# Opening of an expert stage: router products taken from x, ranks in five products, token lists made by one-hot products

## Reference, cut to what matters

```python
def hierarchical_moe(h, w_rg, b_rg, w_re, b_re, w1, w3, w2):
    b, s, d = h.shape
    t = h.reshape(b * s, d)
    p_group = jax.nn.softmax((t @ w_rg + b_rg).astype(jnp.float32), axis=-1)
    g_val, g_idx = lax.top_k(p_group, 1)
    fine = (t @ w_re + b_re).astype(jnp.float32).reshape(-1, N_EXPERT_GROUPS, EXPERTS_PER_GROUP)
    fine_sel = jnp.take_along_axis(fine, g_idx[:, :, None], axis=1)[:, 0]
    e_val, e_idx = lax.top_k(jax.nn.softmax(fine_sel, axis=-1), TOP_K_IN_GROUP)
    ...
    for e in range(N_EXPERTS):
        y_e = (jax.nn.silu(t @ w1[e]) * (t @ w3[e])) @ w2[e]
        out = out + combine[:, e:e + 1] * y_e
```

## Time and profile before

| | us |
|---|---|
| median of 3 runs | 3279.79 |
| lowest and highest | 3277.72, 3288.72 |
| the profiled execution, device time | 3293.47 |
| its span, first to last instruction | 3291.5 |
| mean clock granted to PE in it, share of full speed | 0.939 |
| PE busy, share of the span | 90% |
| DVE, ACT, POOL | 51%, 37%, 5% |

### The profile page before, as it was taken

How to read it: one execution, slowest core, us unless ns; L and a number is a source line. 1 busy time by engine, 2 the same in 40 slices (tenths; PEclk the granted TensorE clock), 3 DMA queues, 4 the chain that set the end, 5 groups by cost and what they waited for, 6 DMA issues and landing times. The chain is left out here.

```text
span 3291.5 us, 37902 instructions
## 1 busy us (share of the span) xinstructions
PE 2946.6 (90%) x14197; PEld 2339.0 (71%) x14197; DVE 1693.6 (51%) x2383; ACT 1212.7 (37%) x1625; POOL 172.2 (5%) x131
## 2 busy tenths in 40 slices
PE   7899989789999899897999999989877878599996
PEld 3674776678888888675777887867655567477775
DVE  5444423644677343434654343352466453588886
ACT  2320222323322232432334442244324322377774
POOL 0000001100011000000000000000000100222220
PEclk9999998899999999997999999999979788799998
DMA  8300110021345142110012222223100023599996
GB/s 353 126 26 13 52 51 1 30 86 66 123 148 179 59 134 96 39 45 16 1 34 88 96 96 70 89 70 89 52 8 1 0 66 140 206 364 358 357 343 237
DMA packets 76312, 362.81 MB, mean 110 GB/s; under 512 B 13428, under 2 KB 17347, under 8 KB 50596
## 3 DMA queue, kind: packets, MB, share of 16 engines
q1 hardware_dynamic: 62404, 327.69, 28.1%
q0 software_dynamic: 13792, 33.58, 3.0%
HBM read 360.68 MB, written 16.27 MB: 115 GB/s over the span
## 5 line engine op out<-in xcount | busy, mean ns | idle before, releaser
L305 PE MATMUL ps<-rounded,rounded 128*128 128x512 f32 (+3 forms) x3700 | 1381.5, 373 | 140.0 <-DVE rounded L2238 23.9
L306 PE MATMUL ps<-rounded,rounded 128*128 128x512 f32 (+3 forms) x3700 | 1341.2, 362 | 0.0
L307 PE MATMUL ps<-rounded,rounded 128*128 128x512 f32 (+3 forms) x3700 | 1338.9, 362 | 0.0
L305 PEld LDWEIGHTS ps<-rounded,rounded 128*128 128x128 f32 (+1 forms) x3700 | 708.6, 192 | 324.5 <-issue 120.9
L307 PEld LDWEIGHTS ps<-rounded,rounded 128*128 128x128 f32 (+1 forms) x3700 | 709.7, 192 | 107.7
L306 PEld LDWEIGHTS ps<-rounded,rounded 128*128 128x128 f32 (+1 forms) x3700 | 710.9, 192 | 94.9
L284 DVE TENSOR_TENSOR rounded<-work,rounded 128x1024 fp32r<-128x1024 f32 (+3 forms) x224 | 306.6, 1370 | 838.5 <-ACT rounded L280 838.3
L280 ACT CAST rounded<-work 128x1024 fp32r<-128x1024 f32 (+3 forms) x224 | 261.0, 1166 | 740.1 <-PE ps L307 627.2
L3470 DVE TENSOR_TENSOR rounded<-work,rounded 128x2048 fp32r<-128x2048 f32 x138 | 309.7, 2286 | 77.9 <-ACT rounded L3315 77.9
L3315 ACT CAST rounded<-work 128x2048 fp32r<-128x2048 f32 x138 | 259.4, 1915 | 80.0 <-PE ps L307 80.0
L291 PE MATMUL ps<-cst 128*128 128x256 f32 x466 | 127.6, 435 | 64.6 <-PEq L171 64.6
(11 more groups left out here) (481 smaller groups left out, 2509.4 us busy)
## 6 DMA issues: line engine op xcount, KB each, us to landing
work<-in_moe SPq DMA_DIRECT2D x138, 1024.0 KB, 7.4
work<-in_ffn_up SPq DMA_DIRECT2D x44, 1024.0 KB, 4.8
work<-in_ffn_down SPq DMA_DIRECT2D x66, 512.0 KB, 3.4
work<-in_ada_w SPq DMA_DIRECT2D x12, 2048.0 KB, 17.9
work<-in_ada_w POOLq DMA_DIRECT2D x48, 512.0 KB, 4.0
work<-in_w_out SPq DMA_DIRECT2D x16, 512.0 KB, 3.6
work<-in_w_gates SPq DMA_DIRECT2D x16, 512.0 KB, 3.6
work<-in_w_in_hy SPq DMA_DIRECT2D x12, 512.0 KB, 3.5
```

What stands on the lines that cost most here:

```text
L305: k.nc.tensor.matmul(out, sh, mh, start=start, stop=False)
L306: k.nc.tensor.matmul(out, sh, ml, start=False, stop=False)
L307: return k.nc.tensor.matmul(out, sl, mh, start=False, stop=stop)
```

## The change

1. Router. The 32 products read x as it lies in SBUF, with the router's weights multiplied by the norm's gain (one DVE operation, semaphore `weighted`); the scale of each token is applied to the 20 results (four operations). `h_turned`, its 32 transposes and 8 copies go.
2. Ranks. Five products over all blocks at once, one with the triangle and four with ones, in place of 14.
3. Lists. DVE marks for each pick its tile (`at_tile`) and its position (`at_pos`) as one-hot matrices; eight products of these, summed in PSUM, are the turned list. The list in HBM, its fill, the eight indirect stores, the load and a transpose go.
4. Order on DVE. The gain rows and the normed rows of blocks 0 and 1 come after the picks, those of blocks 2 and 3 after the matching. The table of overflow tiles is made in the loop ahead of tile 2, the shares ahead of tile 3.
5. ACT rounds the first four chunks before the exponentials. POOL empties all four `picked` places itself, ahead of the gathers. SP waits for the table (`mapped`) only at the first overflow tile and for `indexed` no more.
6. Fillers: 8 ahead of the rank products, 8 after them, 16 after the list products.

```diff
@@ SP
             sp.dma_start(w, k.dram["w_router"]).then_inc(asked, 16)
-            sp.wait_ge(cleared, 1)
-            sp.dma_start(slot_rows, by_tile).then_inc(filled, 16)
...
                 sp.dma_start(k.h_rows[a * P:(a + 1) * P, :], h_tok[:, a, :]).then_inc(stored, 16)
-            sp.wait_ge(spread_out, 16 * 8)
-            sp.dma_start(by_tile, slot_rows).then_inc(listed, 16)
-            sp.wait_ge(indexed, 1)
...
+                    if part == 0 and t == N_EXPERTS:
+                        sp.wait_ge(mapped, 1)
@@ POOL
-            pool.wait_ge(counted, 4)
-            pool.wait_ge(filled, 16)
-            pool.wait_ge(numbered, 1)
-            for c in range(8):
-                pool.indirect_dma_start(k.slot_list, bass.IndirectOffsetOnAxis(ap=slot_no[:, c:c + 1], axis=0),
-                                        token_no[:, c:c + 1], None).then_inc(spread_out, 16)
+            for b in range(2, PICKED):
+                pool.memset(picked[b], 0.0).then_inc(emptied, 1)
+            pool.wait_ge(logit, 1)
+            for b in range(2):
+                pool.memset(picked[b], 0.0).then_inc(emptied, 1)
+            pool.wait_ge(emptied, PICKED)
             pool.wait_ge(indexed, 1)
             pool.wait_ge(stored, 64)
...
-            for b in range(2):
-                gather(b)
-            for b in range(2, PICKED):
-                pool.memset(picked[b], 0.0).then_inc(emptied, 1)
-            pool.wait_ge(emptied, PICKED - 2)
-            for b in range(2, PICKED):
+            for b in range(PICKED):
                 gather(b)
@@ PE
+            pe.wait_ge(weighted, 1)
             pe.wait_ge(tok_kept[0], 2)
-            pe.wait_ge(tok_kept[1], 2)
+            for a in range(4):
+                for d in range(DT):
+                    last = nc.tensor.matmul(k.bank(2, 20, 20 * a), k.x[:, d, CTX + a * P:CTX + (a + 1) * P],
+                                            w[:, d * 20:(d + 1) * 20], start=d == 0, stop=d == DT - 1)
+            last.then_inc(logit, 1)
...
+            keep_running(k, 8, 4)
             pe.wait_ge(chosen, 1)
-            flat = picks.rearrange("p a g e -> p a (g e)")
-            for a in range(5):
-                for b in range(min(a, 3) + 1):
-                    last = nc.tensor.matmul(k.bank(1, 16, 16 * a), k.const("s_le_t") if b == a else every, flat[:, b, :],
-                                            start=b == 0, stop=b == min(a, 3))
+            flat = picks.rearrange("p a g e -> p (a g e)")
+            nc.tensor.matmul(k.bank(6, 64, 64), every, flat, start=True, stop=True)
+            nc.tensor.matmul(k.bank(6, 64), k.const("s_le_t"), flat, start=True, stop=False, skip_group_check=True)
+            for a in range(1, 4):
+                last = nc.tensor.matmul(k.bank(6, 64 - 16 * a, 16 * a), every, flat[:, 0:64 - 16 * a], start=False, stop=a == 3,
+                                        skip_group_check=True)
             last.then_inc(summed, 1)
-            pe.wait_ge(listed, 16)
-            nc.tensor.transpose(k.bank(2, EXPERT_TILES), by_tile, k.cst[0:EXPERT_TILES, CAT["ident"]:CAT["ident"] + EXPERT_TILES]
-                                ).then_inc(list_turned, 1)
+            keep_running(k, 8, 4)
+            pe.wait_ge(matched, 1)
+            for c in range(8):
+                last = nc.tensor.matmul(k.bank(3, EXPERT_TILES), at_pos[:, c, :], at_tile[1][:, c, :], start=c == 0, stop=c == 7)
+            last.then_inc(listed, 1)
+            keep_running(k, 16, 4)
@@ DVE
+            dve.wait_ge(asked, 16)
...
+            V.tensor_tensor(by_part, by_part, gains, ALU.mult).then_inc(weighted, 1)
...
+            dve.wait_ge(gain_spread, 1)
+            V.tensor_copy(gain_rows, k.ps[:, 0:D]).then_inc(gained, 1)
...
+            normed_rows(0, 2)
...
+            link(V.tensor_tensor(beyond, slots.unsqueeze(2).to_broadcast(shape), borders.unsqueeze(1).to_broadcast(shape), ALU.is_ge))
+            link(V.tensor_reduce(tile_of, beyond, AX.X, ALU.add))
+            link(V.tensor_tensor(at_tile[0], beyond[:, :, 0:EXPERT_TILES], beyond[:, :, 1:EXPERT_TILES + 1], ALU.subtract))
+            link(V.scalar_tensor_tensor(out=pos, in0=tile_of, scalar=-1.0 * SLOTS, in1=slots, op0=ALU.mult, op1=ALU.add))
+            link(V.tensor_tensor(at_tile[1], at_tile[0], token_no.unsqueeze(2).to_broadcast([P, 8, EXPERT_TILES]), ALU.mult))
+            V.tensor_tensor(at_pos, pos.unsqueeze(2).to_broadcast([P, 8, SLOTS]),
+                            pos_no.unsqueeze(1).to_broadcast([P, 8, SLOTS]), ALU.is_equal).then_inc(matched, 1)
+            normed_rows(2, 2)
...
+                if t == 2:
+                    map_tiles()
+                if t == 3:
+                    shares()
```

More of the change, by code:

```diff
@@ L3090, in experts @@
     ids, off = room(EXPERT_TILES), room(EXPERT_TILES)
-    by_tile = k.row[0:EXPERT_TILES, 0:SLOTS]
-    slot_no, to_row, from_row, rows_of = (
-        k.whole[:, 0:8], k.whole[:, 8:8 + EXPERT_TILES], k.whole[:, 32:32 + EXPERT_TILES],
+    at_tile = [k.words(at + a * EXPERT_TILES * 8, at + (a + 1) * EXPERT_TILES * 8).rearrange("p (c i) -> p c i", i=EXPERT_TILES)
+               for a in range(2)]
+    at += 2 * EXPERT_TILES * 8
+    beyond = k.words(at, at + 8 * (EXPERT_TILES + 1)).rearrange("p (c i) -> p c i", i=EXPERT_TILES + 1)
+    at += 8 * (EXPERT_TILES + 1)
+    borders, pos_no = k.words(at, at + EXPERT_TILES + 1), k.words(at + EXPERT_TILES + 1, at + EXPERT_TILES + 1 + SLOTS)
+    at_pos = k.words(ring.end, ring.end + 8 * SLOTS).rearrange("p (c s) -> p c s", s=SLOTS)
+    tile_of, pos = room(8), room(8)
+    to_row, from_row, rows_of = (
+        k.whole[:, 8:8 + EXPERT_TILES], k.whole[:, 32:32 + EXPERT_TILES],
         k.whole[:, 56:56 + 6 * OVER].rearrange("p (o c) -> p o c", c=6))
@@ L3206, in _ @@
             last.then_inc(gain_spread, 1)
-            for a in range(4):
-                pe.wait_ge(normed, a + 1)
-                if a == 0:
-                    for h in range(2):
-                        pe.wait_ge(tok_kept[h], 4)
-                for d in range(DT):
-                    last = nc.tensor.transpose(k.bank(d, P, a * P), h_tok[:, a, d * P:(d + 1) * P], ident)
-            last.then_inc(back_turned, 1)
-            pe.wait_ge(asked, 16)
-            for a in range(4):
-                for d in range(DT):
-                    if a == 0:
-                        pe.wait_ge(back_kept[d % 2], d // 2 + 1)
-                    last = nc.tensor.matmul(k.bank(0, 20, 20 * a), h_turned[:, d, a * P:(a + 1) * P],
-                                            w[:, d * 20:(d + 1) * 20], start=d == 0, stop=d == DT - 1)
@@ L3301, in _ @@
             nc.scalar.activation(root, sum_sq, ACT.Sqrt, bias=k.const("eps"), scale=1.0 / D).then_inc(rooted, 1)
-            act.wait_ge(back_turned, 1)
-            for d in range(0, DT, 2):
-                nc.scalar.copy(h_turned[:, d, :], k.bank(d)).then_inc(back_kept[0], 1)
-            act.wait_ge(spaced, 1)
-            nc.scalar.activation(g_exp, g_exp, ACT.Exp).then_inc(raised, 1)
-            act.wait_ge(spaced, 2)
-            nc.scalar.activation(gap, gap, ACT.Exp).then_inc(raised, 1)
             def high(c, n):
@@ L3326, in _ @@
             high(0, ring.SPLIT)
+            act.wait_ge(spaced, 2)
+            nc.scalar.activation(g_exp, g_exp, ACT.Exp).then_inc(raised, 1)
+            nc.scalar.activation(gap, gap, ACT.Exp).then_inc(raised, 1)
             for half in range(2):
@@ L3371, in _ @@
                 V.tensor_copy(x_tok[:, a, 0:512], k.bank(2 * a)).then_inc(tok_kept[0], 1)
-            for b in range(2):
-                V.memset(picked[b], 0.0).then_inc(returned, 1)
-            dve.wait_ge(gain_spread, 1)
-            V.tensor_copy(gain_rows, k.ps[:, 0:D]).then_inc(gained, 1)
-            dve.wait_ge(gained, 1)
             dve.wait_ge(rooted, 1)
@@ L3379, in _, with normed_rows @@
             dve.wait_ge(inverse, 1)
[L3380 to L3389 removed]
+            def normed_rows(a, n):
+                for a in range(a, a + n):
+                    V.scalar_tensor_tensor(out=h_tok[:, a, :], in0=x_tok[:, a, :], scalar=root[:, a:a + 1], in1=gain_rows,
+                                           op0=ALU.mult, op1=ALU.mult).then_inc(normed, 1)
             first = k.const("first").unsqueeze(1).to_broadcast([P, 4, 4])
@@ L3400, in _ @@
             dve.wait_ge(logit, 1)
-            bias = k.vec[:, COL["b_router"]:COL["b_router"] + 20].unsqueeze(1).to_broadcast([P, 4, 20])
-            link(V.tensor_tensor(logits, k.bank(0, 80).rearrange("p (a n) -> p a n", n=20), bias, ALU.add))
+            bias = k.vec[:, COL["b_router"]:COL["b_router"] + 20]
+            for a in range(4):
+                last = V.scalar_tensor_tensor(out=logits[:, a, :], in0=k.bank(2, 20, 20 * a), scalar=root[:, a:a + 1], in1=bias,
+                                              op0=ALU.mult, op1=ALU.add)
+                link(last)
             groups = logits[:, :, 0:4]
@@ L3450, in _ @@
```

(7 more changed lines are left out.)

92 lines of the change are left out of this document (46 added, 46 removed).

## The result

| | before | with the change |
|---|---|---|
| median of 6 runs each, us | 3282.3 (3277.72 to 3301.5) | 3261.03 (3253.51 to 3269.76) |
| ratio, 95% interval | | 0.9916 (0.9888 to 0.9944) |
| profiled execution / its span, us | 3293.47 / 3291.5 | 3258.2 / 3256.1 |
| mean granted clock of the span | 0.939 | 0.948 |

A forecast was written before the change was run, and what follows sets the result against it. TensorE, busy 90% of the span, was taken as the bound, with 67.03 us before the loop begins. Opening −22.6, fillers −0.7 and table +1.0 gave −22.3 us, from median 3279.79 to 3257.5 us; range 3249 to 3270.

The forecast's parts named there:

- Steps 1 to 7: Opening of the last stage, from the first transposes at 2758.27 to the indices ready at 2792.4.
- step 1: Opening: router products directly behind the 3.70 us of transposes, taking 10.89 us, end 2772.9; 12.9 us gone.
- step 3: Picks to ranks: PE gain product 1.88, eight fillers 5.21, rank products 2.2; DVE copy and normed rows 3.6; both end 2782.2.
- Step 6: PE sums the lists with eight products in 2.7 us, end 2791.3, replacing indirect stores, load and one transpose.
- Step 8: Stores of normed rows before the gathers: last takes 3.5 us, lands 2794.5 and releases the gathers; other bound 10.9 us.
- rival B: Opening: stores or gathers meet the weight chunks, stores 7.4 us later; −15 us, 3265; chance 0.13.
- Step 9: First gather: 0.8 us from release to start, 7.36 to the transposes, at 2802.7 instead of 2825.30: −22.6 us.
- Step 10: Start of the loop: 16 more fillers let first transposes and products find the higher clock; −0.7 us, bounds 0 and −2.
- Step 11: Overflow table, 3.76 us on DVE, moves into the loop before the third tile's subtractions; +1.0 us, bounds 0 and 3.8.
- A: PE stays on the lower clock in the opening, ranks 3.5 us later; −17 us, 3263; chance 0.15.
- C: Slower: the loop holds PE at the lower clock after the new opening; two tiles give +15 us, 3295; chance 0.03.
- D: Nothing moves: the loop is bound by transfers (share 0.98) and the last chunk sets the end; 3280; chance 0.03.

The follow-up runs named there:

- the list part alone: Kernel before with only one-hot matrices and eight products in place of the list in HBM; opening 61.0 us, first two tiles 38.4 us.
- the kernel with the table early: Changed kernel with the overflow table made before the loop, between normed rows and indices, not ahead of the third tile; opening 44.1 us, stage 506.6 us.

## Why the prediction was right, and where not

The sum was −22.3 us for the stage, and the profile shows −28.8; the medians moved by −21.3, between runs of one kernel that scatter by 24 before and 16 with the change. The timetable, in us from the start of the stage:

| step | | forecast | measured |
|---|---|---|---|
| 1 | router products done, logits at VectorE | 14.6 | 14.4 |
| 2 | picks | 20.2 | 20.25 |
| 3 | VectorE free for the ranks | 23.9 | 23.8 |
| 4 | slots | 27.3 | 27.1 |
| 5 | matched | 30.3 | 30.1 |
| 6 | list summed | 33.0 | 33.4 |
| 7 | indices | 34.1 | 34.45 |
| 8 | last store landed | 36.2 | 35.3 |
| 9 | first gather starts | 37.1 | 36.2 |
| 9 | first transposes | 44.4 | 42.5 |

**Steps 1 to 7** were right to 0.4 us over 34, most taken from a row of the same shape. Five one-hot operations of 184 to 192 columns or fewer took 0.17 to 0.36 and the wide one 1.22, the value of a normed row. Part of it is luck. In step 1 the clock: 10.73 us of router products where the same shape took 8.4 to 12.8 elsewhere. In step 3 two sizes were off and cancelled: the gain product took 3.40 us and not 1.88, the fillers 3.62 and not 5.21. Step 6 was 0.4 late in all, because the list products ran at 0.50 from 2784 on:

```profile
2780.00:2782.00 2.00, 0.09 (x1) 0.10 (x1) 1.90 (x5) 0.00 (x0) 0.00 (x0) 1.00 0.00 0
2782.00:2784.00 2.00, 2.00 (x12) 2.00 (x12) 2.00 (x2) 0.00 (x0) 0.00 (x0) 0.60 0.07 27
2784.00:2786.00 2.00, 2.00 (x9) 1.82 (x9) 0.97 (x5) 0.00 (x0) 0.00 (x0) 0.50 1.00 406
```

(columns as in the earlier trace rows: stretch, busy PE, PEld, DVE, ACT, POOL, clock, DMA share, GB/s).

**Step 8** was mis-sized: 2.7 us for a store, not 3.5; rival B's 10 us did not come, since no chunk was in the queue. Its bold sentence, that the stores release the gathers, is true of the start of the first issue and false of its end, which is what counts: where the issue begins inside the first subtraction, as here, it ends 0.9 to 1.0 behind it.

**Step 9** kept the 7.36 of before. The span from gather start to transposes is no constant: it holds the wait for the subtraction and the traffic of the chunk that SP asks for behind it. In the kernel before the gather started 0.9 after the subtraction did, the issue took 2.30 and the transfer 5.06; with the change it started 1.8 after it, and the two took 1.45 and 4.80, thus 6.25. The earlier start (0.9) and the shorter span (1.1) are the 2.0 us by which the opening was better than forecast. Where the issue was not held and less of a chunk, or none, was on its way, the span was 4.3 to 5.0.

**Step 10** forecast −0.7 by the fillers; the first tile gave −3.1, but over two tiles the kernel without fillers reached nearly as much (38.3 against 38.1, before 41.1). The size was off by 2.3, and its cause was not the one named: the list part alone, with no filler, gave 2.7 of it, and by what means is open.

**Step 11** forecast +1.0, measured +0.3: the slack behind the 2.29 us of idle time was larger than half a microsecond.

**The tail** had no term and gave −1.5: the chain's last load of the output rows took 10.16 us where it took 11.92:

```profile
3240.39 10.16 DMA work<-y_rows
3250.64 1.29 DVE h L3516
```

Nothing in the change bears on it, and over the runs the tail was 30.4 to 32.2.

Sum of misses: −2.0 opening, −2.3 first two tiles, −0.7 table, −1.5 tail, thus −6.5. The profiled execution was 6.5 better again in the code ahead of the stage: 3258.2 where 3293.47 − 22.3 = 3271.2 was forecast for it. Against that, I took 13.7 us off to come from the profiled execution to the median, and with the change the median lies 2.8 above the profiled execution: 16.5 too much. 16.5 − 13.0 = 3.5, and 3261.03 is 3.5 above 3257.5. The number was right because these errors cancelled; the difference between a profiled execution and the median is no constant, since the code ahead of the stage alone moves by more.

**Rivals.** A (lower clock in the opening) came in part: in the gain product, where it cost nothing, in the list products, and in the loop's second tile. B, C and D did not: stores 2.7 us, clock 1.00 between 2900 and 3000, and the whole opening arrived at the end, since loop times past the third tile are those of before to 0.05 us.

## What to carry to other kernels

Before a chain of GpSimd gathers is moved, look at what VectorE does at that moment: an issue that begins inside a large two-input VectorE operation ends about 1 us behind it, so such an operation should be over, or begin with the issue and not before it. Look as well at which large loads that operation releases, since a 1 MB chunk asked for just ahead of the gather made it land 1.7 us later. Take the duration of a PE step of few columns as a range over the two clocks, and give the fillers a place where the step behind them is short of its clock and not where the next data may land under them. When the part is 1% of a program whose unchanged part scatters by as much, measure the stage between marks and not the run.

## What was not expected of the hardware

- The 64 rows of 128x20 products took from 8.4 to 12.8 us, by how much of them ran at a granted clock of 0.50. With the same instructions ahead of them they took 10.9 in both profiles of the kernel before and 12.7 to 12.8 in two other kernels.
- Fillers ahead of the gathered tokens gave the full clock at once and a fall in the second tile (22.07); without fillers, after 9.28 us of idle PE, the clock was back after some five products and did not fall in the second tile (20.49). The fall is not tied to fillers: it came without any in the kernel before (22.02) and stayed away with all of them in the kernel with the table early (20.48).
- The issue of a gather of 128 rows takes 0.99 to 1.12 us, also where a subtraction of 2048 columns with two SBUF inputs begins with it or behind it; where it begins inside such a subtraction it ends 0.86 to 1.00 us after that one, and takes up to 2.66. The subtraction takes 2.28 to 2.32 us either way.
- From the end of the issue the rows of a gather land in 3.1 us with no weight chunk on its way, and in 4.8 to 5.1 with one of 1 MB asked for 0.8 to 1.0 us before.
- Store of 512 KB to HBM: 2.6 to 2.7 us into an empty queue, 10.1 to 10.9 beside weight chunks.
